# Order of the first transfers in a convolutional decoder layer: two x tiles in flight, first weights at once, convolution state last

## The reference

```python
u = _rmsnorm(h, g_mix)
proj = jnp.einsum('ntd,de->nte', u, w_in)          # 1024 -> 9216
a_b, a_c, a_h, a_z, b_v, b_g, b_z, gate_a, gate_b = jnp.split(proj, SPLITS, axis=-1)
# branch A: short gated convolution, 3 taps; sample tokens continue from state_conv_a
ya = (a_b * dwconv3(a_c * a_h) * silu(a_z)) @ w_out_a
# branch B: GLU -> dwconv31 -> LayerNorm -> swish, gated
v = b_v * sigmoid(b_g)
yb = (silu(layernorm(dwconv31(v) + b_conv_b)) * silu(b_z)) @ w_out_b
h = h + (sigmoid(gate_a) * ya + sigmoid(gate_b) * yb) @ w_o
h = h + sigmoid(rmsnorm(h) @ w_pg) * (p @ w_pe)
y = rmsnorm(h, g_final)
```

## Time and profile before

| | |
|---|---|
| time, median of 3 runs | 862.86 us (861.85 to 863.13) |
| span of the profiled execution, slowest core (4) | 861.8 us |
| spans of the 8 cores | 855.7 to 861.8 us |
| PE busy | 837.3 us, 97% |
| DVE / ACT / POOL busy | 478.1 / 304.0 / 216.1 us |
| HBM read / written | 169.26 / 17.25 MB |
| matmuls of the projections (L582, on uT) | 536.9 us |

### The profile page before, as it was taken

The page is one execution under the profiler, slowest core; times in us unless marked ns, Lnnn a source line. Parts: engine busy times, 40 slices in busy tenths (PEclk is TensorE's granted clock), DMA queues, the critical chain, the costliest instruction groups (busy, mean ns, idle before and its releaser), DMA issues.

```text
span 861.8 us, 16560 instructions; the slowest of 8 cores (855.7 to 861.8 us)
## 1 busy us (share of the span) xinstructions
PE 837.3 (97%) x5746; PEld 498.3 (58%) x5790; DVE 478.1 (55%) x676; ACT 304.0 (35%) x426; POOL 216.1 (25%) x402
## 2 busy tenths in 40 slices
PE   7899999999999999999899999999999999999995
PEld 3677777777777777775344444444444444444442
DVE  3545576766856742344776244555566483234566
ACT  3212232322344531434565212222224342242554
POOL 3532332332312111122442222222221221000121
PEclk9999999999999999999999999999999999999998
DMA  9999999999969864799998998998987899353533
GB/s 242 163 195 184 198 157 162 162 170 162 153 100 208 117 98 74 161 232 152 220 274 213 157 154 124 148 146 130 147 140 121 171 167 168 52 159 61 142 100 108
DMA packets 88826, 133.44 MB, mean 155 GB/s; under 512 B 37272, under 2 KB 45736, under 8 KB 86696
## 3 DMA queue, kind: packets, MB, share of 16 engines
q0 software_dynamic: 33392, 57.72, 44.7%
q1 hardware_dynamic: 55208, 74.40, 39.6%
q10 hardware_dynamic: 144, 0.26, 0.1%
HBM read 169.26 MB, written 17.25 MB: 216 GB/s over the span
## 4 chain that ended last, share of the span: by engine, by line
PE 86%; DMA 4%; DVE 4%; ACT 3%; issue 2%; SPq 0%; POOL 0%; DVEq 0%; POOLq 0%; ACTq 0%
PE ps L582 72%; PE ps L1060 5%; PE ps L1004 5%; PE ps L720 3%; DMA t_xs<-x 2%; PE ps L1052 1%; DMA t_ring<-w_in 1%; ACT t_tmp L414 1%; DVE t_cbuf L1015 1%; ACT t_tmp L738 1%; DMA t_u2T<-t_xb 1%; ACT t_cbuf L1074 1%; DVE t_tmp L861 0%; ACT t_xb L1020 0%; DVE t_uT L559 0%
## 5 line engine op out<-in xcount | busy, mean ns | idle before, releaser
L582 PE MATMUL ps<-t_uT,t_ring 128*128 128x288 bf16 (+1 forms) x3429 | 536.9, 316 | 6.0 <-DVE t_uT L559 2.2
L582 PEld LDWEIGHTS ps<-t_uT,t_ring 128*128 128x128 bf16 x3456 | 336.1, 98 | 200.5 <-issue 10.2
L394 POOL DMA_DIRECT2D t_ring<-w_in x144 | 79.1, 550 | 300.5 <-PE ps L582 279.1
L938 ACT ACTIVATE t_tmp<-ps 128x576 f32<-128x576 f32 (+1 forms) x48 | 36.7, 771 | 107.5 <-PE ps L582 107.5
L946 DVE SCALAR_TENSOR_TENSOR t_tmp<-t_tmp,ps 128x576 f32<-128x576 f32 (+1 forms) x27 | 24.6, 910 | 86.1 <-PE ps L582 86.1
L1060 PE MATMUL ps<-t_reg,t_u2T 128*128 128x512 bf16 x267 | 62.7, 386 | 3.4 <-DMA t_u2T<-t_xb 2.6
L582 PE MATMUL ps<-t_yaT,t_ring 128*128 128x288 bf16 (+1 forms) x383 | 61.7, 317 | 0.1
L582 PE MATMUL ps<-t_cbuf,t_ring 128*128 128x288 bf16 (+1 forms) x382 | 61.5, 317 | 0.1
L1004 PE MATMUL ps<-t_cbuf,t_yaT 128*128 128x512 bf16 x267 | 60.7, 379 | 0.3
L905 DVE TENSOR_TENSOR t_tmp<-ps,t_tmp 128x576 f32<-128x576 f32 (+1 forms) x24 | 21.8, 912 | 60.0 <-PE ps L582 60.0
L644 DVE SCALAR_TENSOR_TENSOR t_vta<-t_tmp,ps 128x512 bf16<-128x512 f32 (+1 forms) x24 | 20.7, 863 | 58.2 <-ACT t_tmp L641 50.7
(11 more groups left out here) (115 smaller groups left out, 804.1 us busy)
## 6 DMA issues: line engine op xcount, KB each, us to landing
t_ring<-w_in POOLq DMA_DIRECT2D x144, 256.0 KB, 6.9
t_xs<-x SPq DMA_DIRECT2D x30, 512.0 KB, 6.6
y<-t_cbuf SPq DMA_DIRECT2D x16, 512.0 KB, 3.8
t_reg<-vd SPq DMA_DIRECT2D x32, 132.0 KB, 5.5
t_reg<-vd SPq DMA_DIRECT2D x32, 131.9 KB, 5.9
t_reg<-vd SPq DMA_DIRECT2D x32, 131.9 KB, 6.8
t_reg<-vd SPq DMA_DIRECT2D x32, 131.9 KB, 7.6
t_ring<-w_cv POOLq DMA_DIRECT2D x16, 256.0 KB, 9.0
```

What stands on the lines that cost most here:

```text
L394: S.add("pool", lambda e, k=k, src=src: e.dma_start(out=ring[k][:, :], in_=src), writes=[f"ring{k}"], dma=f"ring{k}")
L582: S.add("pe", lambda e, k=k, si=si, c0=c0: e.matmul(ps[:, b + si, 0:wb], lhsT=ring[k_][:, 128 * k:128 * k + 128], rhs=src[:, k, c0:c0 + wb ...
L938: S.add("act", lambda e: e.activation(out=two(tg), in_=pp(bg), func=AF.Tanh, scale=0.5), reads=pres(bg), writes=[tgr])
```

## The change

SP's list: x2 to x7 now name the tile two places ahead as read (x2 names x0, x3 names x1, and so on), so that SP waits for its landing before it issues the next. `hista` moves from ahead of x8 to behind it. GpSimd's list: w0 and w1 both stand ahead of the statistics of x0; w2 moves from behind the statistics of x3 to behind those of x2, w3 from behind those of x4 to behind those of x3. What comes after is as before. No data and no other instruction change.

```diff
--- before.py
+++ after.py
@@ -478,17 +478,18 @@
                 if i < NXS + 4 else (xw[0], "xs0")
             x0.append((t, nm))
 
-        def x0load(i):
+        def x0load(i, after=None):
             t, nm = x0[i]
             r = tiles_of(0)[i]
             S.add("sp", lambda e: e.dma_start(out=t, in_=x_d[r:r + 128, :].rearrange("t (h m) -> t h m", h=2)),
+                  reads=[] if after is None else [x0[after][1]],
                   writes=[nm], dma=f"x0{nm}" if i < NXS + 4 else "xs0")
 
         x0load(0)
         S.add("sp", lambda e: e.dma_start(out=vecs[:], in_=vecs_d), writes=["vecs"], dma="vecs")
-        for i in range(1, NXS + 4):
-            x0load(i)
-        S.add("sp", lambda e: e.dma_start(out=hista[:], in_=sa_d), writes=["hista"], dma="hista")
+        x0load(1)
+        for i in range(2, NXS + 4):
+            x0load(i, i - 2)
         S.add("dve", lambda e: e.memset(mhalf[:], -0.5), writes=["mhalf"])
         S.add("dve", lambda e: e.memset(yaT[:, 0, 0:640], 0.0), writes=["fz"])
         for i in range(2):
@@ -1163,11 +1164,11 @@
                 def turn(i, b):
                     s1_turn(i, xo[i % 4], b)
 
-                pump(1)
+                pump(2)
                 s1_sq(0)
-                pump(1)
                 sc(0)
                 x0load(NXS + 4)
+                S.add("sp", lambda e: e.dma_start(out=hista[:], in_=sa_d), writes=["hista"], dma="hista")
                 fill(20)
                 turn(0, 4)
                 s1_sq(1)
@@ -1175,13 +1176,13 @@
                 fill(12)
                 turn(1, 5)
                 s1_sq(2)
+                pump(1)
                 sc(2)
                 fill(12)
                 turn(2, 6)
                 s1_sq(3)
                 pump(1)
                 s1_sq(4)
-                pump(1)
                 sc(3)
                 sc(4)
                 fill(6)
```

## The result

The changed kernel takes 869.77 us (median of four runs) against 863.0 us for the kernel before. In one of the four (1036.77 us) the cores of one half of the chip ran at a granted clock of 0.81, and such runs are left out of every ratio and mean here; the other three took 868.77 to 870.41 us. The ratio is 1.0071, 95% interval 1.0053 to 1.009, so the kernel is slower by 6.1 us by the ratio. The forecast was 863.4 with a range to 865.2. The case on the slow side named the right place and had 865.2 to 866.3 for it; even that was too small.

The account below looks back on a forecast made before the run. TensorE's matmuls bound it, busy 837.3 of 861.8 us. The terms put x8's landing, and so the head, +0.3 us later on core 4, up to +1.3 on core 1; taking +0.5 gave 863.4 us, range 860.4 to 865.2.

Parts of the forecast that it names:

- case on the slow side: ScalarE's queue, tanh behind x8's square: all of w4 ahead of x8, 865.2 us, with throttle 866.3; chance 0.25.
- the gate: Start of x5's transposes, after 29.3 us: opens at the later of x8's landing + 3.0 us and w3's + 1.3.
- the state is free: SP's queue: the state's 0.38 us transfer moves behind x8; nobody reads it before 49.5 us.
- w3's 1.40 us wait: TensorE at 28.22 us on core 4: with w2 and w3 issued earlier, this wait for w3 goes.
- (a): SP's queue: x2 to x7 wait for the tile two ahead; costs one microsecond or less, at most 0.22 us a tile.
- the sum: x8's landing: w3 +1.0, w4 +0.7, state -0.4, so +1.3 us, less 1.0 saved by fewer tiles in flight.
- The weights get in front of x8: ScalarE's tanh behind x8's square: more weights move before x8, +2.3 us, 865.2, with throttle 866.3; chance 0.25.
- The 1.0 us that I set against it: x8's landing on core 4: fewer x tiles in flight save 1.0 of the 3.8 us lost in the head.
- (e): TensorE's head on core 4: x1's transposes start at 12.1 and not 14.00, first real matmul 2.0 us earlier.
- a rival had it: Block transition, 400 to 440 us: a shifted head changes how DMA meets there, up to 3.3 us either way; faster 0.10.

## Why the prediction was wrong

**What bounds the kernel, and the gate: right.** The head's end is set by the x5 transposes, and those by x8's landing + 3.0 us; it held on core 1 of after and in the means of seven kernels of the table (32.3 to 35.3, 33.1 to 36.1, 28.6 to 31.6, 29.2 to 32.2 and so on), and moving x7 and x8 out of the way moved it to x6. Also right: no matmul gains from w1, the state is free, w3's 1.40 us wait goes on core 4, though w3 lands at 26.7 there and not before 26.

**(a), the price of the throttle: wrong, and it is the step that failed.** "The throttle costs at most 0.22 us a tile where x runs alone ...; where weights share the engines it costs nothing, since they fill the hole." It came from x0's 3.5 us, the latency of the first transfer, with nothing ahead of it. In pairs a tile takes 7.3 us on the mean in after, so two in flight give one per 3.6 us. The waits alone move x8 by 7.4 us (25.7 to 33.1), where I had 1.1, and the sum that gave the forecast left out even that. Some 4 of these are the waits: 0.9 us a tile without weights and not 0.22, and by estimate 0.8 with weights, where I had put nothing. Most of the rest is weights (2.8 us on core 4) that got ahead of x8 because it had become late; the sum has 1.7 us of weights, and only for their earlier issue. The hole was filled, as I said, but with bytes that stand ahead of x8. A nearer row was there: x1, with one tile ahead of it, took 8.6 us on core 4 and 6.6 on core 1, which for two in flight is a tile per 3.3 to 4.3 us.

The Trainium skill's fixed cost plus bytes (DMA: Bandwidth & Descriptors, "Anatomy of one DMA — SWDGE (gpsimd) path") gave an estimate of 3.2 us a tile. The page has that fit for transfers issued by GpSimd, and the x tiles are issued by SP. In the trace of before x0 takes 3.3 to 4.5 us on the eight cores (3.5 on core 4), near it; the tiles in pairs with weights beside them take 3.9 to 10.8, up to 3.4 times as much.

**"The weights get in front of x8": right in kind, half its size.** I had +1.3 us net for x8; without any throttle it is +2.9 to +3.5 (the early weights, and w2 and w3 alone), all from w2 and w3. The 1.0 us that I set against it, saved because fewer x tiles are in flight, did not come: with the waits alone x1 lands at 9.4 on the mean, as before, and x2 and x3 a little later.

**(e), the first transposes: right for x1 on core 4, wrong behind it.** There x1's start at 12.63 and not 14.00. On the mean over the cores they start at 13.3 and had started at 12.9, since x1 lands at 9.9 and not 9.4. And the first matmul, which I had 2.0 us earlier, comes 2.1 us later (20.4 against 18.3), because x2 lands 1.9 us later (14.3 against 12.4). Neither half of the change does this alone: x2 lands at 12.6 with the waits alone, and the first matmul comes at 18.4 there and at 18.3 with the early weights alone. It comes only where w1 is issued at once and x2 waits for x0.

**The clock: missing from the sum.** In the head of before, the longest idle time ahead of TensorE's instructions was about 2 us. With 4.5 to 7.4 us of it the granted clock fell (0.98 to 1.01 us for eight transposes on all eight cores), worth 1.5 us on the mean at the head. It fell with shorter waits too: with the early weights alone, where TensorE waits 1.4 to 3.9 us ahead of these transposes, the granted clock from 31 to 38 us is 0.56 to 0.76 on six of the eight cores. My sum had no term for the clock at all.

**The sum with measured terms,** as means over the cores: gate +6.0 (29.3 to 35.3), clock and what comes with it +1.6 (16.7 against 15.0 from gate to head mark): head +7.6 us. The spans of the profiled executions grow by 6.4 on the mean over the cores (858.7 to 865.1), the time by 6.1. The 1.2 us between 7.6 and 6.4 show at the transition: in its 40 us TensorE is busy for 38.4 us on the mean before and 39.6 in after. The two slowest cores of before had lost 3.3 and 3.2 us there; in after core 1 is busy for 38.57, and loses 1.4. The transition did move, as a rival had it, with the good sign, and was too small to matter against 7.6.

## What to carry to other kernels

A wait for a landing costs what a transfer takes under load, divided by the number in flight, and not what it takes in an empty machine: so take the issue-to-landing time of a transfer that had as many beside it as the throttled ones will have, and not that of the first one. Here four tiles of 512 KB were enough and two were not. And whatever runs beside a throttled queue fills the hole with its own bytes, which then stand ahead of the last transfer. Before any transfer is moved forward, find the instruction that stands behind the last one in some engine's list; here ScalarE's tanh stood behind the square of the ninth tile, and the same early weights cost 0.37% with it and gained 0.19% without.

## What was not expected of the hardware

- Full issue queues were worth more than order: with a full queue and x alone the tiles came at 1.5 us each, in pairs with nothing beside them at 2.4 with a DMA share of 0.6 to 0.8, in pairs beside the weights at 3.5.
- Early weights in the throttled kernel are no loss (x8 at 32.3 and not 33.1) and in the free-running one they land x8 2.9 us later. The DMA share with and without weights beside the waiting tiles (0.90 and 0.64) shows that weights fill what the waits leave idle; that this is why the early ones are no loss there is argued and not shown.
- Filling a 5 us gap with matmuls kept the clock at 1.00 on seven of eight cores and gave 1.5 us at the head, of which nothing reached the slowest core.
